# Neighbourhood attention: the values of four pairs of heads at once, by seven products of halves, with the modulation rows loaded singly and moved

## The chip, the cores and the metric

The kernel runs on one core of a Trainium2 chip, in one launch, all in float32. The core has a matrix engine (TensorE, PE in the profile; PEld is its loading of weights), a vector engine (VectorE, DVE), a scalar engine (ScalarE, ACT), GpSimd (unused here but for start-up) and SyncE (SP), whose queue issues every DMA of the kernel. Operands lie in the on-chip memory SBUF; TensorE writes to eight PSUM banks of 128 x 512. The metric is the device time of one launch in microseconds, the median of the timed runs.

## The reference

Two DiT-like layers and a third block on 256 latent tokens and 256 context tokens, width 1024. The change lies in the mixer of the second layer, which attends from each latent query to a grid window and to all context tokens:

```
def na_mixer(h, hc, w_qkv, rpb, w_o, need_ctx):
    H, d = 16, 64
    q = (h @ w_qkv[:, :1024])                       # latent tokens only
    k, v   = split((h  @ w_qkv[:, 1024:]), 2)       # 256 latent tokens
    kc, vc = split((hc @ w_qkv[:, 1024:]), 2)       # 256 context tokens
    s     = q k^T * d**-0.5 + bias(rpb), masked to the window
    s_ctx = q kc^T * d**-0.5
    p = softmax([s_ctx, s])
    y = (p[:ctx] @ vc + p[ctx:] @ v) @ w_o
```

Beside it, the kernel computes rows of the modulation (`ada_w`, a matrix times the conditioning vector c after SiLU) for later layers; 32 of these rows, each a dot product of 1024 with the 128 columns on the partitions, are done by VectorE in this stage.

## The kernel before

SBUF holds `A`, the layer input, transposed: 128 partitions x 8 steps of k (KT) x 512 tokens (T; columns 0 to 255, CTX, are context, the rest latent, LAT). Weights come through a ring of two slots of 6144 columns, filled by SP in the order of the table `STREAM`; a chunk may overwrite the chunk two before it when the semaphore in `CHUNK_USED` says so. SP's program (`sync_program`, `load_pairs`) is one queue in order: a wait in it holds up every issue behind it.

The stage `na_heads` goes over 8 pairs of heads (`NA_PAIRS`). Each pair has one chunk of 3072 columns: its query, key and value weights. TensorE's order (`na_heads_pe`, from L2158) is, for pair u: `scores(u)` (L2120, four products of 512 columns with 64 rows), `values(u)` (through the helper `mm`, L593: four tiles of 128 tokens, eight steps of k each, 128 columns wide), `keys(u+1)` (L2086, eight steps of 512 columns), `turn(u)` (L2127, 16 transposes of the normalized probabilities), `queries(u+1)` (L2082, eight steps of 256 columns) and `attend(u)` (L2138). In pair 0 half of the values stands ahead of the scores. In pair 7 there are no next keys; 12 products of the output projection (`out`, L2145) stand in their place, and two more behind `turn`. A float32 product counts as two instructions in the profile.

VectorE (`na_heads_dve`) does, for each pair: `maxima` (masking the bias, L2194; scaling the scores and adding the bias, L2204 and L2205; the maximum, L2209 and L2211), `normalize` (L2218, L2221), up to four or five modulation rows (`far`, L2229), two copies of turned tiles (`na_turned`, L2253), the copy of the next queries (L2186) and the copy of the attended output (L2245). ScalarE (`na_heads_act`) does the exponentials (L2268), copies values and keys out of PSUM (L2271, L2262) and copies two turned tiles. Everything is ordered by semaphores; `attend(u)` waits for both engines' copies of the turned tiles.

The modulation rows of this stage are loaded two at a time (`FAR_EACH`), 1024 KB, into three buffers (`load_far`, L420), each when the rows that were in the buffer are used. `FAR_PER_PAIR` says how many rows VectorE does in which pair. The biases of all 16 heads, 4 MB, lie in `N` and come in two parts (`load_biases`, L441), the first ahead of the second pair's chunk.

The stage before it (`ffn_split`) and others already compute products of two halves by seven in place of eight smaller products: sums and differences of blocks of the input and of the weights are formed by VectorE, seven products are made, and partial results are copied out of PSUM between products.

## Time and profile before

| | us |
|---|---|
| median of 3 timed runs | 1899.43 (1898.46 to 1900.1) |
| the profiled execution: its run | 1898.38 |
| the profiled execution: its span | 1896.5 |
| TensorE busy in the span | 1741.8 (92%), 14306 instructions |
| VectorE busy | 915.5 (48%) |
| ScalarE busy | 367.2 (19%) |
| mean granted TensorE clock | 0.969 |
| HBM read | 393.26 MB, mean 209 GB/s |

The page divides the span into 40 slices. TensorE is busy nine tenths or more from the second slice to the thirtieth, and six to eight tenths in the expert stage at the end, in which the DMA engines are busy throughout and the granted clock is 0.8. The neighbourhood attention lies in slices 16 to 20, from 715.6 to 908 us. Its products are known by their lines in the kernel, which the table of groups, the chain of waits and the timelines all name.

### The profile page before, as it was taken

The page shows a single profiled execution, that of the slowest core. Times are in us where ns is not written, and L with a number is a line of the kernel's source. Part 1 is how long each engine was busy: PE and PEld are TensorE (multiplying, and loading weights), DVE is VectorE, ACT ScalarE, POOL GpSimd, SP SyncE. Part 2 cuts the span into 40 slices and gives each one's busy share as a digit, 9 for nine tenths or more (in the row PEclk, how much of TensorE's full clock was granted, in tenths as well). Part 3 has the DMA queues.
Part 4 walks back from the last instruction along what each step waited for, and adds up shares of the span by engine and source line. Part 5 has one row for each costly group of instructions (what it writes and reads, how often), then busy time and mean ns, then how long its engine had stood idle before and what let it go on. Part 6 is the DMA issues. An engine that isn't in the chain of part 4 may idle for free.

```text
span 1896.5 us, 33550 instructions
## 1 busy us (share of the span) xinstructions
PE 1741.8 (92%) x14306; PEld 1370.3 (72%) x14306; DVE 915.5 (48%) x1948; ACT 367.2 (19%) x872; POOL 0.2 (0%) x4
## 2 busy tenths in 40 slices
PE   8999999999999999999999999999999876666666
PEld 4455687888888887777888888788888655445554
DVE  1488878666666426677544413478433211111112
ACT  0343413112110114222211102203422100000001
POOL 0000000000000000000000000000000000000000
PEclk9999999999999999999999999999999988888888
DMA  9523342222222217445334543313286999999997
GB/s 383 206 112 139 129 178 88 82 79 81 81 101 86 90 46 221 156 160 196 123 140 171 194 183 134 134 68 134 89 366 265 426 429 427 429 427 430 427 429 310
DMA packets 32947, 395.77 MB, mean 209 GB/s; under 512 B 3664, under 2 KB 6736, under 8 KB 9040
## 3 DMA queue, kind: packets, MB, share of 16 engines
q1 hardware_dynamic: 32848, 394.33, 52.0%
q8 instruction: 77, 1.26, 0.3%
q14 instruction: 22, 0.18, 0.0%
HBM read 393.26 MB, written 1.05 MB: 208 GB/s over the span
## 4 chain that ended last, share of the span: by engine, by line
PE 77%; DMA 18%; DVE 3%; issue 1%; ACT 1%; SPq 0%; DVEq 0%
PE bank L593 22%; PE bank L1873 13%; DMA ring<-w_moe 13%; PE bank L1582 8%; PE bank L646 5%; DMA arena<-w_moe 4%; PE bank L3347 3%; PE bank L2086 3%; PE bank L891 2%; PE bank L3113 1%; PE bank L2082 1%; PE bank L1192 1%; PE bank L800 1%; DMA ring<-w_ada 1%; PE bank L2440 1%; PE bank L1168 1%
## 5 line engine op out<-in xcount | busy, mean ns | idle before, releaser
L593 PE MATMUL bank<-layer_input,ring 128*128 128x256 f32 x1152 | 253.1, 380 | 0.0
L593 PEld LDWEIGHTS bank<-layer_input,ring 128*128 128x128 f32 x1152 | 217.3, 190 | 31.5 <-issue 2.7
L3347 PE MATMUL bank<-arena 128*32 128x128 f32 x2008 | 80.0, 325 | 50.1 <-DMA arena<-w_moe 49.6
L1582 PE MATMUL bank<-arena,ring 128*128 128x256 f32 x544 | 121.8, 380 | 1.1 <-DMA ring<-w_ffn_out 1.1
L1873 PE MATMUL bank<-arena 128*128 128x256 f32 x504 | 115.7, 379 | 0.0
L3499 DVE TENSOR_TENSOR arena<-arena,bank 128x128 f32<-128x128 f32 x32 | 9.2, 288 | 220.5 <-PE bank L3347 220.5
L1582 PEld LDWEIGHTS bank<-arena,ring 128*128 128x128 f32 x544 | 103.1, 190 | 15.8 <-DMA ring<-w_ffn_out 1.5
L3347 PEld LDWEIGHTS bank<-arena 128*32 128x32 f32 x2008 | 68.4, 131 | 61.8 <-DMA arena<-w_moe 58.9
L1873 PEld LDWEIGHTS bank<-arena 128*128 128x128 f32 x504 | 95.7, 190 | 13.2 <-DVE arena L2002 0.2
L646 PE MATMUL bank<-arena,ring 128*128 128x256 f32 x452 | 99.1, 380 | 0.8 <-DVE arena L2245 0.6
L646 PEld LDWEIGHTS bank<-arena,ring 128*128 128x128 f32 x452 | 85.5, 190 | 13.3 <-issue 1.0
L3347 PE MATMUL bank<-ring,arena 128*32 128x128 f32 x1920 | 68.0, 301 | 28.3 <-DMA ring<-w_moe 27.5
L593 PE MATMUL bank<-arena 128*128 128x128 f32 (+2 forms) x400 | 86.5, 370 | 2.2 <-DVE arena L3327 1.0
L3347 PEld LDWEIGHTS bank<-ring,arena 128*32 128x32 f32 x1920 | 58.6, 121 | 38.8 <-DMA ring<-w_moe 33.8
L593 PE MATMUL bank<-ring,layer_input 128*128 128x128 f32 (+2 forms) x576 | 80.9, 300 | 0.0
L593 PEld LDWEIGHTS bank<-ring,layer_input 128*128 128x128 f32 x576 | 69.8, 192 | 14.4 <-issue 13.4
L1873 PE MATMUL bank<-layer_input,ring 128*128 128x256 f32 x336 | 79.4, 379 | 0.0
L593 PEld LDWEIGHTS bank<-arena 128*128 128x128 f32 x400 | 56.3, 193 | 27.3 <-issue 26.5
L1873 PEld LDWEIGHTS bank<-layer_input,ring 128*128 128x128 f32 x336 | 63.8, 190 | 9.1 <-issue 0.5
L3464 DVE COPY arena<-bank 32x256 f32<-32x256 f32 x60 | 24.9, 415 | 88.5 <-PE bank L3358 88.1
L3464 ACT COPY arena<-bank 32x256 f32<-32x256 f32 x60 | 21.8, 363 | 215.2 <-PE bank L3358 214.8
L1935 DVE SCALAR_TENSOR_TENSOR arena<-arena,vectors 128x510 f32<-128x510 f32 x84 | 59.2, 747 | 5.1 <-DVE arena L1931 2.4
(507 smaller groups left out, 2662.9 us busy)
## 6 DMA issues: line engine op xcount, KB each, us to landing
arena<-w_moe SPq DMA_DIRECT2D x45, 2048.0 KB, 25.8
ring<-w_moe SPq DMA_DIRECT2D x45, 2048.0 KB, 26.6
ring<-w_ffn_in SPq DMA_DIRECT2D x22, 2048.0 KB, 7.8
ring<-w_ffn_out SPq DMA_DIRECT2D x8, 2816.0 KB, 9.9
ring<-w_proj SPq DMA_DIRECT2D x7, 3072.0 KB, 10.0
ring<-w_ada_late SPq DMA_DIRECT2D x8, 2560.0 KB, 9.1
ring<-w_na_pair SPq DMA_DIRECT2D x8, 1536.0 KB, 6.2
arena<-w_far SPq DMA_DIRECT2D x11, 1024.0 KB, 6.7
```

The costliest lines, as they stand in the source:

```text
L593: last = pe.matmul(out, a, b, start=(k == 0), stop=(k == len(lhs) - 1))
L646: last = eng.matmul(bank[oc % 2][:, 0:w], self.ring[g % 2][:, o:o + P], rhs(k), start=(k == 0), stop=(k == nk - 1))
L800: last = pe.matmul(out[32 * g:32 * g + 32, 0:n], cs[:, k, :], weights[:, k * width + g * n:k * width + (g + 1) * n], start=(k == 0), stop= ...
L891: ins = pe.matmul(bank[m][:, :], v["w_in"][:, (k * 6 + m) * P:(k * 6 + m + 1) * P], self.A[:, k, :], start=(k == 0), stop=(k == KT - 1))
L1168: pe.matmul(bank[2 + 2 * t + j][:, :], q[half[j], at], k[half[j], :], start=True, stop=False, skip_group_check=True)
L1192: last = pe.transpose(bank[n][:, i * P:(i + 1) * P], p[:, at:at + P], ident)
L1582: last = eng.matmul(out, w[:, k * P:(k + 1) * P], x[:, k, :], start=(start and k == 0), stop=(stop and k == half - 1), skip_group_check=True)
L1873: last = pe.matmul(out, w[:, k * P:(k + 1) * P], x[:, k, :], start=(start and k == 0), stop=(stop and k == 3), skip_group_check=True)
L1935: last = dve.scalar_tensor_tensor(out=seg(u[x], olo, ohi), in0=seg(src[x], ilo, ihi), scalar=self.V[:, bass.ds(cw + t * 2 * FT + col, 1)], ...
L2086: return pe.matmul(bank[1][:, :], slot(u)[:, D + k * P:D + (k + 1) * P], self.A[:, k, :], start=(k == 0), stop=(k == KT - 1))
L3347: ins = eng.matmul(bank[x][group[q], 0:P], xe[:, k, SLOTS * e:SLOTS * e + SLOTS], weight(e, first, last, (x * KT + k) * FE + q * P, P), st ...
L3464: last = copy(y[group[g], (g - e) % 4, :], bank[2][group[g], 0:256])
```

## The change

The values of four pairs are computed at once, as a product of all 512 tokens with 512 columns of weights. Tokens are split in context and latent, k in its lower and upper four steps, columns in two halves of 256 (two pairs each). With the input blocks A11, A12 (context, lower and upper k), A21, A22 (latent) and the weight blocks alike, VectorE forms four sums of the input (s1 to s4, once) and four of the weights (t1 to t4, for each group); TensorE makes seven products of four steps of k, 128 tokens and 256 columns, for each of two token tiles i and each of two groups g: `value(g, i, n)`. ScalarE copies partial results out of the bank between products (`snap`), and VectorE adds three combinations (`cross`, `far_right`). The 14 products of a group are spread over TensorE's order: those of the first group in pair 0, those of the second in pairs 1 to 4. The old `values` is gone, and with it ScalarE's copy of it.

The weights come in six chunks of 4096 columns (2048 KB) in place of eight of 3072: keys and queries of pairs 0 and 1, values of the first group, keys and queries of 2 and 3, values of the second group, then pairs 4 and 5, and 6 and 7. The modulation rows are loaded singly (512 KB) into four buffers, and done 12, 0, 4, 7, 5, 2, 2, 0 in pairs 0 to 7. The biases are held for 8 heads at a time: 2 MB behind the second chunk, and twice 1 MB inside the stage. The turned tiles go to banks 3 to 6, since bank 7 holds products.

The core of the diff:

```diff
-FAR_BUFFERS, FAR_EACH = 3, 2
-FAR_PER_PAIR = (0, 4, 4, 4, 5, 5, 5, 5)
+FAR_BUFFERS, FAR_EACH = 4, 1
+FAR_PER_PAIR = (12, 0, 4, 7, 5, 2, 2, 0)
...
-          ("na_pair", NA_PAIRS, 3072), ("na_o", 2, 4096),
+          ("na_pair", 6, 4096), ("na_o", 2, 4096),
...
+NA_VALUES = {"products_done": OPENED["products_done"] + len(HEAD_STEPS[0]),
+             "scalar_out": OPENED["scalar_out"] + len(HEAD_STEPS[2]),
+             "vector_in": OPENED["vector_in"] + 8 + 4 * 3, "vector_out": OPENED["vector_out"] + 4}
+VALUE_ORDER = [(0, 1), (0, 2), (0, 3), (0, 4), (0, 5), (0, 6), (1, 2), (0, 7), (1, 3), (1, 1), (1, 5), (1, 4), (1, 6), (1, 7)]
+VALUE_STEPS = len(VALUE_ORDER)
...
-    "na_pair": ("na_proj_done", each(1)), "na_o": ("y_ready", each(4, RESIDUAL_BASE["na_o"])),
+    "na_pair": ("na_qk_done", lambda c: 4 * c - 4), "na_o": ("y_ready", each(4, RESIDUAL_BASE["na_o"])),
...
-                if name == "na_pair" and first == 1:
-                    self.load_biases(sp, slice(0, 4), self.const_in)
...
+                    self.load_biases(sp, 0, slice(0, 8), self.const_in)
                     sp.wait_ge(self.sem("ffn0_up_used"), FT + 4)
-                    self.load_biases(sp, slice(4, 16), self.rest_in)
                     self.load_pairs(sp, load, g0)
...
+        values = NA_VALUES["products_done"]
+        chunk("na_qk_done", 4, 2)
+        rows(4, 12)
+        chunk("products_done", values + VALUE_STEPS, 3)
+        rows(12, 16)
+        sp.wait_ge(self.sem("na_biased"), 8)
+        self.load_biases(sp, 8, slice(0, 4), self.rest_in)
+        rows(16, 18)
+        chunk("na_qk_done", 8, 4)
+        rows(18, 20)
+        sp.wait_ge(self.sem("na_biased"), 16)
+        self.load_biases(sp, 8, slice(4, 8), self.rest_in)
+        rows(20, 28)
+        chunk("products_done", values + 2 * VALUE_STEPS, 5)
+        rows(28, FAR_LOADS)
...
+        def value(g, i, n):
+            w, at = self.na_value_weights(g), self.na_steps(g, i)
+            near, far = slice(i * P, i * P + P), slice(CTX + i * P, CTX + i * P + P)
+            low, high, far_high = self.A[:, 0:4, near], self.A[:, 4:8, near], self.A[:, 4:8, far]
+            s1, s2, s3, s4 = [x[:, :, near] for x in v["sums"]]
+            x, y, out, start = {1: (low, "lo0", left, True), 2: (high, "hi0", first_cross, True),
+                                3: (s1, "t1", second_cross, True), 4: (s2, "t2", left, False),
+                                5: (s4, "hi1", second_cross, False), 6: (s3, "t3", left, False),
+                                7: (far_high, "t4", left, False)}[n]
+            if (i, n) == (0, 1):
+                self.na_value_loaded(pe, g)
+            if n in (3, 4, 5, 6, 7):
+                pe.wait_ge(s["vector_in"], ready + ((0, 0, 0, 2, 4, 5, 7, 8), (0, 0, 0, 9, 10, 10, 11, 12))[g][n])
+            if n == 1 and (g, i) != (0, 0):
+                pe.wait_ge(s["scalar_out"], at["free"])
+            if n == 2 and (g, i) != (0, 0):
+                pe.wait_ge(s["vector_out"], at["pair_free"])
+            if n in (4, 5, 6, 7):
+                pe.wait_ge(s["scalar_out"], at[{4: "first", 5: "fifth", 6: "second", 7: "third"}[n]])
+            for k in range(4):
+                last = pe.matmul(out, x[:, k, :], w[y][:, k * CTX:(k + 1) * CTX], start=(start and k == 0), stop=(k == 3),
+                                 skip_group_check=True)
+            last.then_inc(s["products_done"], 1)
...
+        value(0, 0, 1)
+        value(0, 0, 2)
+        scores(0)
+        keys(1)
+        value(0, 0, 3)
+        value(0, 0, 4)
+        value(0, 0, 5)
+        queries(1)
+        value(0, 0, 6)
+        value(0, 1, 2)
+        turn(0)
+        value(0, 0, 7)
+        value(0, 1, 3)
+        value(0, 1, 1)
+        value(0, 1, 5)
+        value(0, 1, 4)
+        keys(2, 0, 3)
+        value(0, 1, 6)
+        keys(2, 3, 5)
+        value(0, 1, 7)
+        keys(2, 5, KT)
+        attend(0)
+        scores(1)
+        queries(2)
+        value(1, 0, 1)
+        value(1, 0, 2)
+        value(1, 0, 3)
+        keys(3, 0, 1)
+        turn(1)
+        value(1, 0, 4)
+        attend(1)
+        scores(2)
+        keys(3, 1, KT)
+        value(1, 0, 5)
+        value(1, 0, 6)
+        turn(2)
+        queries(3)
+        attend(2)
+        scores(3)
+        value(1, 1, 2)
+        keys(4)
+        value(1, 0, 7)
+        turn(3)
+        value(1, 1, 3)
+        queries(4)
+        value(1, 1, 1)
+        value(1, 1, 5)
+        attend(3)
+        scores(4)
+        value(1, 1, 4)
+        keys(5, 0, 5)
+        value(1, 1, 6)
+        keys(5, 5, KT)
+        value(1, 1, 7)
+        turn(4)
+        queries(5)
+        attend(4)
+        for u in (5, 6):
             scores(u)
-            values(u, (2, 3) if u == 0 else range(4))
-            if last:
-
-                pe.wait_ge(self.w_loaded[go % 2], 16 * (go // 2 + 1))
-                pe.wait_ge(s["o_used"], u)
-                out(0, range(KT - 1))
-                out(1, range(KT - 3))
-            else:
-                keys(u + 1)
+            keys(u + 1)
+            queries(u + 1, 0, 4)
             turn(u)
-            if last:
-                out(1, range(KT - 3, KT - 1))
-            else:
-                queries(u + 1)
+            queries(u + 1, 4, KT)
             attend(u)
+        scores(7)
+        pe.wait_ge(self.w_loaded[go % 2], 16 * (go // 2 + 1))
+        pe.wait_ge(s["o_used"], 7)
+        out(0, range(KT - 1))
+        out(1, range(KT - 3))
+        turn(7)
+        out(1, range(KT - 3, KT - 1))
+        attend(7)
...
+        def weight_sum(g, n, count):
+            w = self.na_value_weights(g)
+            if n == 1:
+                self.na_value_loaded(dve, g)
+            if n == 4:
+                dve.wait_ge(s["products_done"], self.na_value_done(g, 1, 2))
+            x, y = {1: ("lo1", "lo0"), 2: ("hi1", "t1"), 3: ("hi1", "lo1"), 4: ("hi0", "t2")}[n]
+            add(w[f"t{n}"], w[x], w[y], ALU.subtract, count)
...
+        def cross(g, i):
+            at, home = self.na_steps(g, i), self.na_value_homes(v, g, i)
+            dve.wait_ge(s["products_done"], self.na_value_done(g, i, 5))
+            dve.wait_ge(s["scalar_out"], at["second"])
+            if g == 1:
+                dve.wait_ge(s["o_done"], 2)
+            dve.tensor_tensor(home["c11"], bank[7][:, 0:CTX], v["first"], ALU.add).then_inc(s["vector_out"], 1)
+            dve.tensor_tensor(home["c12"], bank[7][:, CTX:2 * CTX], v["second"], ALU.add).then_inc(s["vector_out"], 1)
+        def far_right(g, i):
+            at, home = self.na_steps(g, i), self.na_value_homes(v, g, i)
+            dve.wait_ge(s["scalar_out"], at["third"])
+            dve.tensor_tensor(home["c22"], v["third"], v["fifth"], ALU.add).then_inc(s["vector_out"], 1)
...
+        dve.wait_ge(self.sem("mix_a_ready"), self.a_base + KT)
+        add(s1, A[1][0], A[1][1], ALU.add, 1)
+        weight_sum(0, 1, 2)
+        add(s2, s1, A[0][0], ALU.subtract, 3)
+        weight_sum(0, 2, 4)
+        maxima(0)
+        add(s4, A[0][1], s2, ALU.subtract, 5)
+        weight_sum(0, 3, 6)
+        add(s3, A[0][0], A[1][0], ALU.subtract, 7)
+        normalize(0)
+        cross(0, 0)
+        fars(0, 0, 1)
+        queries(1)
+        weight_sum(0, 4, 8)
+        fars(0, 1, 2)
+        turned(0)
+        far_right(0, 0)
+        fars(0, 2, 6)
+        cross(0, 1)
+        fars(0, 6, 8)
+        far_right(0, 1)
+        fars(0, 8, 12)
+        attended(0)
+        maxima(1)
+        weight_sum(1, 1, 9)
+        normalize(1)
+        weight_sum(1, 2, 10)
+        turned(1)
+        weight_sum(1, 3, 11)
+        queries(2)
+        attended(1)
+        maxima(2)
+        normalize(2)
+        cross(1, 0)
+        fars(2, 0, 2)
+        turned(2)
+        far_right(1, 0)
+        fars(2, 2, 4)
...
+        for u in (5, 6):
             maxima(u)
             normalize(u)
-            for i in range(min(FAR_PER_PAIR[u], 4)):
-                far(sum(FAR_PER_PAIR[:u]) + i)
-            self.na_turned(u, 0, s, v, dve, dve.tensor_copy, "pt_dve")
-            if FAR_PER_PAIR[u] > 4:
-                far(sum(FAR_PER_PAIR[:u]) + 4)
-            if u + 1 < NA_PAIRS:
-                queries(u + 1)
-            dve.wait_ge(s["o_done"], u + 1)
-            dve.tensor_copy(v["oT"][:, u * LAT:(u + 1) * LAT], bank[6][:, 0:LAT]).then_inc(s["o_used"], 1)
+            fars(u, 0, 2)
+            turned(u)
+            queries(u + 1)
+            attended(u)
+        maxima(7)
+        normalize(7)
+        turned(7)
+        attended(7)
...
+        snap(0, 0, "first")
+        keys(1)
+        snap(0, 0, "fifth")
+        soften(0)
+        snap(0, 0, "second")
+        act.wait_ge(self.cvec_in, 96)
+        act.activation(self.far_c(), self.far_c(), ACT.Silu).then_inc(self.sem("open_silu_ready"), 1)
+        snap(0, 0, "third")
...
-    W["na_pair"] = a["na_w_qkv"][0].reshape(KT, P, 3, NA_PAIRS, P).transpose(3, 1, 2, 0, 4)\
-        .reshape(NA_PAIRS, P, -1)
+    w = a["na_w_qkv"][0].reshape(KT, P, 3, NA_PAIRS, P)
+    qk = w[:, :, 0:2].reshape(KT, P, 2, 4, 2, P).transpose(3, 1, 4, 2, 0, 5).reshape(4, P, -1)
+    vw = w[:, :, 2].reshape(2, 4, P, 2, 2, CTX).transpose(3, 2, 0, 4, 1, 5).reshape(2, P, -1)
+    W["na_pair"] = np.stack([qk[0], vw[0], qk[1], vw[1], qk[2], qk[3]])
```

In ScalarE's order, the exponentials `soften(u)` and the copies `keys`, `turned` stand as before with the copies `snap` between them. `add` is one VectorE sum and a wait for it.

## Rows read from the trace of the kernel before

**Rows 1.** Windows: core, us, busy us (instructions) by engine, granted clock, DMA share, GB/s.
```profile
715.60:912.00 196.40, 195.43 (x1130) 140.84 (x1131) 137.71 (x270) 53.67 (x114) 0.00 (x0) 1.00 0.50 178
```

**Rows 2.** Chain of waits in the stage: start us, us, engine, line, instructions.
```profile
726.27 3.57 PE bank L593 x32
729.84 1.92 PE bank L2120 x8
731.75 3.77 PE bank L593 x32
735.52 6.87 PE bank L2086 x16
742.39 1.75 PE bank L2127 x16
744.14 3.46 PE bank L2082 x16
747.59 1.88 PE bank L2138 x16
...
751.39 7.34 PE bank L593 x64
```

**Rows 3.** Timeline of TensorE, first FFN: start us, us, engine, line, operation.
```profile
404.36 1.89 PE L1873 MATMUL bank<-arena 128*128 128x256 f32 x8
406.09 1.89 PE L1873 MATMUL bank<-layer_input,arena 128*128 128x256 f32 x8
```

**Rows 4.** VectorE's groups by form: line, operation, shapes, count, busy us, mean ns, idle.
```profile
L2229 DVE CUSTOM_DVE_ANT_0 arena<-arena,ring,vectors 128x1024 f32<-128x1024 f32 x22 | 27.3, 1280 | 0.0
...
L2765 DVE TENSOR_TENSOR residual<-arena 128x1024 f32<-128x1024 f32 x8 | 9.7, 1218 | 5.3 <-PE bank L2524 4.0 <-PE bank L2530 1.3
```

**Rows 5.** Timeline of TensorE, pair 7: scores and attend.
```profile
888.65 1.99 PE L2120 MATMUL bank<-arena 64*128 64x512 f32 x8
...
905.90 1.95 PE L2138 MATMUL bank<-arena 128*64 128x256 f32 x16
```

**Rows 6.** Timeline of VectorE, pair 7: the normalizing, then the copies.
```profile
897.49 0.88 DVE L2221 TENSOR_SCALAR arena<-arena,stats 128x512 f32<-128x512 f32 x2
...
898.89 0.88 DVE L2221 TENSOR_SCALAR arena<-arena,stats 128x512 f32<-128x512 f32 x2
...
904.52 1.28 DVE L2253 COPY arena<-bank 128x512 f32<-128x512 f32 x2
```

**Rows 7.** DMA issues: out<-in, queue, count, KB each, median us to landing.
```profile
ring<-w_ffn_in SPq DMA_DIRECT2D x22, 2048.0 KB, 7.8
...
arena<-w_far SPq DMA_DIRECT2D x11, 1024.0 KB, 6.7
```

**Rows 8.** DMA of w_ffn_in alone, its 22 issues.
```profile
DMA to landing us min/median/max: 7.5/7.8/8.6
```

**Rows 9.** DMA of w_na_o alone, its 2 issues.
```profile
DMA to landing us min/median/max: 8.8/9.8/10.7
```

**Rows 10.** Timeline of the DMA queue: issue us, us (of both), line.
```profile
881.41 0.33 SPq L420 DMA_DIRECT2D arena<-w_far  x1
881.78 16.55 SPq L328 DMA_DIRECT2D ring<-w_na_o  x2
```

**Rows 11.** Timeline of TensorE, expert stage and ahead of it; idle us before, releaser.
```profile
1452.24 3.81 PE L593 MATMUL bank<-arena 128*128 128x128 f32 x32 [1.05 <-DVE arena L3327]
...
1568.72 3.45 PE L3358 MATMUL bank<-arena 128*32 128x256 f32 x32 [2.14 <-DMA arena<-w_moe]
...
1578.43 2.94 PE L3347 MATMUL bank<-ring,arena 128*32 128x128 f32 x64 [2.94 <-DMA ring<-w_moe]
```

**Rows 12.** Windows of one us in the expert stage, columns as in rows 1.
```profile
1568.00:1569.00 1.00, 0.28 (x8) 0.24 (x12) 0.00 (x0) 0.00 (x0) 0.00 (x0) 0.99 1.04 442
1569.00:1570.00 1.00, 1.00 (x16) 0.68 (x12) 0.00 (x0) 0.00 (x0) 0.00 (x0) 0.50 1.08 459
...
1572.00:1573.00 1.00, 0.88 (x8) 0.54 (x4) 0.77 (x2) 0.73 (x2) 0.00 (x0) 0.80 0.92 393
```

More of the change, by code:

```diff
@@ new lines, in na_heads_dve, with add @@
+        ready_0 = NA_VALUES["vector_in"]
+        A = [[self.A[:, 4 * y:4 * y + 4, c:c + CTX] for y in range(2)] for c in (0, CTX)]
+        s1, s2, s3, s4 = v["sums"]
+        def add(out, x, y, op, count):
+            dve.tensor_tensor(out, x, y, op).then_inc(ready, 1)
+            dve.wait_ge(ready, ready_0 + count)
+        def weight_sum(g, n, count):
[6 more added lines that the diff above has]
+            add(w[f"t{n}"], w[x], w[y], ALU.subtract, count)
@@ new lines, in na_heads_dve @@
+        normalize(1)
[11 more added lines that the diff above has]
+        fars(2, 2, 4)
+        queries(3)
+        attended(2)
+        maxima(3)
+        weight_sum(1, 4, 12)
+        normalize(3)
+        fars(3, 0, 2)
+        turned(3)
+        fars(3, 2, 5)
+        queries(4)
+        fars(3, 5, 7)
@@ L2262, in keys, with soften @@
             act.copy(v[f"k{u % 2}"], bank[1][:, :]).then_inc(s["k_copied"], 1)
[L2263 to L2264 removed]
+        def soften(u):
             _, nb, rs, _ = v["stats"][u % 2]
```

197 lines of the change are left out of this document (136 added, 61 removed).

## The prediction

> **What bounds the kernel now.** The profiled execution spans 1896.5 us and its run took 1898.38 us; the median of the three timed runs is 1899.43 us, 1.05 us above it. I work out a difference and take it off the median. The change lies in one stage, the neighbourhood attention, so I read that stage and not the shares of the whole. First the table of windows [rows 1]: from 715.6 to 912 us TensorE is busy 195.43 of 196.40 us, at full clock (1.00, which is the 2.4 GHz level), while VectorE is busy 137.71 us. Then the chain of waits [rows 2]: from 726.27 us on it is TensorE work laid end to end, with no engine or DMA between. So the stage is as long as its TensorE instructions. A pair of heads takes 23.2 us: scores 1.92, values 7.34, keys 6.87, turn (the transposes) 1.75, queries 3.46, attend 1.88 [rows 2]. Whatever shortens TensorE's list is a full gain as long as nobody makes it wait. That second half is the question here, since the 7.34 us of values were also what TensorE did while the softmax of the pair ran on VectorE and ScalarE.
>
> **What is removed.** Values of pairs 0 to 7: 3.57 + 3.77 for pair 0 and 7 x 7.34 us for the others [rows 2], the same in each pair: 58.7 us for 256 products of 128 columns.
>
> **What is added on TensorE.** Per group of four pairs, 7 products x 2 token tiles x 4 steps of k = 56 products of 256 columns; two groups, 112. The kernel already has such products of four steps with a wait ahead of each: two of them start at 404.36 and 406.09 us, 1.73 us apart, or 0.432 us for one step [rows 3]. 28 x 1.73 = 48.4 us. TensorE's list gets 10.3 us shorter. Queries and keys keep their number and shape. From here I lay the new lists of the three engines beside each other, in the order of the diff, with these durations, and start TensorE's first value product at 726.2 us. The same walk over the old order ends attend of pair 7 at 907.9 us; in the trace it starts at 905.90 and lasts 1.95 us [rows 5].
>
> **What is added on VectorE.** Four sums of halves of the input and eight of the weights, 128x1024 each: 12 x 1.22 us, as the nearest form takes [rows 4], with a wait behind each some 1.27. Twelve combinations of 128x256, about 0.4 us each. Together 20 us on an engine that has 59 us free in the stage, so the total is no bound; the places are what counts. In pair 0 VectorE copies the queries (726.8), makes four sums (731.9), the maxima (738.5), three sums (742.3), so that t1, t2, s4, s3 are ready at 729.4, 731.9, 739.8 and 742.3 us. TensorE wants them at 738.5, 740.2, 741.9 and 747.1 us. It has scores and the keys of pair 1 ahead of them, and waits for none. The last weight sum (t4) ends at 751.9 us and is wanted at 752.3: cover 0.4 us, and if it goes, the wait costs what it is late. Priced at nothing, kept with +-0.5.
>
> **The modulation rows.** Still 32, of 1.2 us each when they follow one another (22 of them were busy 27.3 us) [rows 4], 12 of them now in pair 0, where TensorE has 47 us of work (14 value products, two keys, scores, queries, turn, attend). VectorE is done with them at 770.9 us and attend of pair 0 ends at 773.2. Each is loaded alone, at 512 KB, where a 1024 KB row load took 6.7 us in the median [rows 7]; the fourth later row is needed more than 3.9 us after its issue in my walk, and VectorE has 2.3 us to spare at the end. Nothing for TensorE. In pairs 5 and 6 two rows stand between the softmax and VectorE's copies of the turned tiles. There the cover is gone: normalizing ends 11.1 us after the scores start (888.65 to 899.77) [rows 5, 6], two rows make 13.5, the two copies (1.28 us together from 904.52) [rows 6] make 14.9, and attend may start at 15.0. TensorE is there at 1.92 + 6.87 + 3.46 + 1.75 = 14.0. **A wait of 0.9 us, twice.** With values it was 21.3.
>
> **Pair 7** has nothing in place of its values but the 12 early products of the output projection, 5.2 us. The first normalized tile comes 9.3 us after the scores start (888.65 to 897.97), the last 11.1 [rows 5, 6]; TensorE is at turn after 1.92 + 5.2 = 7.1. It waits 2.1 us, then 0.6 inside turn. Less the 0.2 us that the old order waits before its last attend: **+2.5 us.**
>
> **The loads.** Weights now come as 2048 KB chunks, at fewer places. SP issues in order, so I follow its queue. Chunk 0 and the first value chunk are asked for before the stage, the latter now ahead of the biases; the copy of c, biases and rows behind it are 4.5 MB where there were 7.5 MB. Chunk 2 is issued at 747.2 (queries of pair 1 done) and needed at 761: hidden. The second value chunk, issued 768.8, needed 778.6 by TensorE: hidden, by 9.7 against 7.8. **Chunk 4 is not.** It waits for the queries of pair 3, and between their end and the keys of pair 4 TensorE has only attend 1.88, scores 1.92 (0.2 late for the copy of the queries) and one product of 1.73, 5.7 us. A 2048 KB load took 7.8 us in the median of 22 [rows 7], 7.5 to 8.6 [rows 8]; 8.8 and 10.7 in the two of the output weights [rows 9], the first of which is issued 0.4 us behind a row load [rows 10]. With 7.8 and 0.1 us for SP and TensorE each the wait is **2.6 us**, and 0.2 at the scores; with 8.8 it is 3.6, with 10.7 5.5. I take 7.8 since the two rows ahead of chunk 4 are issued 3.6 and 2.4 us before it and are 512 KB only. Chunk 5 is issued at about 850.0, behind a row load and the last product of the second group, and wanted at 858.9: 8.9 us, hidden at 7.8, 1.8 us of wait at 10.7. Biases of pairs 4 to 7 are issued 50 us before their use. The Trainium skill ("DMA: Bandwidth & Descriptors", Anatomy of one DMA) fits one DMA as 2.0 us and the bytes at 436 GB/s; that makes 6.8 us here, an estimate by that page, and by it the wait would be 1.6 and the gain 1.0 us larger. The rows, 22 of them at 7.5 or more, decide for the longer time.
>
> **The clock.** The old stage has no gap. The new one has one of 2.6 us before the keys of pair 4 and one of 2.1 (with 0.6 close behind) in pair 7. What a gap does is seen in the expert stage: TensorE had stood for 2.14 us at 1568.72 and for 2.94 at 1578.43 [rows 11]; around the first the granted clock was 0.99 in the microsecond from 1568 and 0.50 in the one from 1569 (the 1.2 GHz level), with 0.80 in that from 1572 [rows 12], so low for some 3.4 us, in which half the work is lost: 1.7 us. The 1.05 us before 1452.24 [rows 11] are the nearest gap on the other side, and TensorE had worked densely up to it. 2.6 and 2.1 are nearer to the longer gaps, but the work ahead of those is thinner than here. I count one such stretch, +1.7, with 0 and 3.4 as bounds.
>
> **The sum.** -10.3 + 2.6 + 0.2 + 1.8 + 2.5 = -3.2 us without the clock, -1.5 with one low stretch. 1899.43 - 1.5 = 1897.9 us. The own range of this case is 1895.5 to 1900.5.
>
> **Rivals.** A measurement of this kernel tells about 0.2% (3.8 us) from no change.
> (1) *The clock holds.* Then 1899.43 - 3.2 = 1896.2. For it: dense products around the gap. Against: both gaps of [rows 11] over 2 us. It is within 0.2% too.
> (2) *The chunks come late, and it is slower.* SP's queue holds row loads ahead of chunks 4 and 5 and rows behind. If they cost as [rows 9] shows at its long end, 10.7 us, the waits are 5.5 (keys of pair 4), 2.2 (keys of pair 6), 1.4 (first product of the second group), 0.4 at scores, 0.9 and 2.5: 12.9, a loss of 2.6 us, and with two or three low stretches 6 to 8: about 1905.5. It decides from a landing of 9.8 us on (9.3 with one low stretch). Against it: the rows ahead are half as large as the one in front of that row.
> (3) *The waits are mostly not there.* If chunk 4 is hidden and the rows of pairs 5 and 6 cost nothing, only pair 7's 2.5 is left: 1899.4 - 7.8 = 1891.6. For it: none of the new waits is in the trace, and my walk has some 90 places where a landing or a copy can come sooner than I count. Against: 5.7 us of cover is less than the shortest of the 22 landings, 7.5.
> (4) *The products don't run at 0.432.* The old values take 7.34 / 32 = 0.229 us for 128 columns, 0.459 for 256. At that pace 112 products take 51.4 us, the gain on the list is 7.3 in place of 10.3, and the time 1900.9. Against: [rows 3].
>
> **Chances.** Forecast with one low stretch 0.42, (1) 0.22, (2) 0.12, (3) 0.14, (4) and other added waits of some us 0.10. Faster by over 0.2% is (3) and the lucky end of (1): 0.18. Slower by over 0.2% is (2) and a little of (4): 0.12. Within: 0.70. The range takes in forecast, (1), (4) and the bounds of landing and clock: 1894.9 to 1901.9.
>
> **What would show it.** In the new trace: value products 1.73 us apart per four steps; keys of pair 4 waiting for a DMA of na_pair, 2.6 us; attend of pairs 5 and 6 waiting 0.9 us for VectorE's copies; turn of pair 7 waiting 2.1 us for VectorE; a granted clock of 0.50 for some us behind the keys' wait or not; no wait for a sum in pair 0; everything after the stage shifted by one amount. The prediction is wrong if the 2048 KB loads land in other than 7.5 to 8.8 us, if VectorE falls behind in pair 0, or if a wait stands at a product that I counted as covered.

## The result, and the profile after

The changed kernel takes 1902.07 us (median of 20 runs, 1900.58 to 1905.76), the kernel before 1898.66 us (20 runs beside them): ratio 1.0016, 95% interval 1.001 to 1.0022. It is slower by some 3.4 us where -1.5 us were forecast, and its time is 0.2 us above the upper end of the range of the forecast. The profiled execution spans 1899.5 us (before 1896.5).

The page of the changed kernel: TensorE's busy time (PE), and the granted clock by slice.

```profile
PE 1734.4 (91%) x14018; PEld 1357.6 (71%) x14018; DVE 932.5 (49%) x1972; ACT 370.3 (19%) x884; POOL 0.2 (0%) x4
...
PEclk9999999999999999999999999999999988888888
```

TensorE is busy 7.4 us less in the whole span and the span is 3.0 us longer. The windows of the stage, which answer to [rows 1]:

```profile
714.70:912.00 197.30, 188.09 (x835) 125.39 (x836) 154.28 (x292) 56.76 (x126) 0.00 (x0) 0.99 0.52 172
```

In place of 1 us TensorE now stands 9.2 us, and the clock is 0.99 instead of 1.00. The timeline of TensorE (start us, us, line, shapes, in brackets the wait ahead and who ended it) shows the new products and every wait of 0.2 us or more up to the output projection:

```profile
746.29 1.89 PE L2188 MATMUL bank<-ring,arena 128*128 128x256 f32 x8
748.01 1.89 PE L2188 MATMUL bank<-ring,layer_input 128*128 128x256 f32 x8
...
785.26 1.09 PE L2207 MATMUL bank<-constants,arena 128*128 128x128 f32 x8 [0.25 <-DVE arena L2362]
786.79 1.99 PE L2188 MATMUL bank<-ring,arena 128*128 128x256 f32 x8 [0.43 <-DVE ring L2391]
...
817.06 8.83 PE L2145 MATMUL bank<-layer_input,ring 128*128 128x512 f32 x16 [3.90 <-DMA ring<-w_na_pair]
...
876.04 1.95 PE L2221 MATMUL bank<-arena 128*64 128x256 f32 x16 [0.73 <-DVE arena L2500]
...
892.89 1.95 PE L2221 MATMUL bank<-arena 128*64 128x256 f32 x16 [0.72 <-DVE arena L2500]
...
904.13 1.09 PE L2207 MATMUL bank<-constants,arena 128*128 128x128 f32 x8 [1.99 <-DVE arena L2362]
905.54 1.09 PE L2207 MATMUL bank<-constants,arena 128*128 128x128 f32 x8 [0.32 <-DVE arena L2362]
```

From top to bottom: two value products 1.72 us apart; two waits in pair 1 that nobody had forecast; the keys of pair 4 behind the DMA of chunk 4, and 8.83 us long instead of 7.13; attend of pairs 5 and 6; the two halves of the turn of pair 7. I measure the stage from here on between the first value product and the first product of the output projection: **182.36 us before (726.10 to 908.46), 184.78 after (725.22 to 910.00)**. Summed by kind, from each group's start to the next one's less the wait (an instruction that waits inside a group counts with the group):

| us in the stage | before | after | 
|---|---|---|
| values | 58.09 | 49.10 |
| keys | 48.07 | 50.37 |
| turns | 13.99 | 14.68 |
| scores, queries, attend, output products | 61.60 | 61.67 |
| waits | 0.61 | 8.96 |
| sum | 182.36 | 184.78 |

So +2.4 us come from the stage. The start of the stage lies 0.9 us earlier, which is within the scatter (725.2 to 727.0 in the profiles of the changed kernel and its variants), and the time behind it is 988.04 us before and 989.50 after; that difference is looked at behind the experiments.

Windows of one us from 817 us on, behind the wait of 3.90 us (the column behind the last "(x0)" is the granted clock):

```profile
817.00:818.00 1.00, 0.94 (x2) 0.49 (x3) 0.47 (x2) 1.00 (x5) 0.00 (x0) 0.94 1.18 365
818.00:819.00 1.00, 1.00 (x2) 0.34 (x1) 0.96 (x3) 1.00 (x3) 0.00 (x0) 0.50 0.95 152
...
821.00:822.00 1.00, 1.00 (x3) 0.38 (x3) 1.00 (x3) 0.00 (x0) 0.00 (x0) 0.85 1.05 238
```

The clock is 0.50, the 1.2 GHz level, from 818 to 821 us and 0.85 in the next one; the keys take 1.70 us more. In pair 7, behind 1.99 us of standing, it stays 1.00.

SP's queue around chunk 4 (issue us, us, line), and what it loaded (KB each, us to landing):

```profile
803.60 1.54 SPq L424 DMA_DIRECT2D arena<-w_far  x2
807.47 0.33 SPq L334 DMA_DIRECT2D ring<-w_na_pair  x1
807.84 1.24 SPq L424 DMA_DIRECT2D ring<-w_far  x2
...
ring<-w_na_pair SPq DMA_DIRECT2D x1, 2048.0 KB, 9.5
```

And pair 1 on ScalarE:

```profile
779.87 0.37 ACT L2527 COPY extra<-bank 128x256 f32<-128x256 f32 x1 [8.64 <-PE bank L2188]
780.26 1.28 ACT L2514 ACT_TABLE_LOAD   x1
781.55 0.72 ACT L2514 ACTIVATE arena<-arena,stats 128x512 f32<-128x512 f32 x1
```

The maxima of pair 1 are ready at 779.45 us (VectorE, L2352). ScalarE stands before its copy of the first product of the second group, comes to the exponentials behind it, and only then loads their table, 1.28 us: the first exponential starts at 781.55, 2.1 us late. In the kernel before nothing stood ahead of the exponentials, and the table was loaded at 747.15 us while ScalarE waited for the maxima.

### The profile page after: what moved, and what is told of

It reads as the page before. It is cut to its first block, busy times and chain, and to the rows that moved or that the text cites. A ratio compares the mean times of both kernels' runs of the same rounds, so it can differ in the third digit from the quotient of the medians.

```text
span 1899.5 us, 33068 instructions
## 1 busy us (share of the span) xinstructions
PE 1734.4 (91%) x14018; PEld 1357.6 (71%) x14018; DVE 932.5 (49%) x1972; ACT 370.3 (19%) x884; POOL 0.2 (0%) x4
## 4 chain that ended last, share of the span: by engine, by line
PE 74%; DMA 20%; DVE 4%; ACT 1%; issue 1%; SPq 0%; DVEq 0%; ACTq 0%
PE bank L615 19%; DMA ring<-w_moe 18%; PE bank L1895 13%; PE bank L1604 9%; PE bank L668 5%; PE bank L3647 3%; PE bank L2188 2%; PE bank L2145 2%; PE bank L913 2%; PE bank L3413 1%; PE bank L2141 1%; PE bank L1214 1%; DMA ring<-w_ada 1%; PE bank L822 1%; PE bank L2740 1%; PE bank L1190 1%
## 5 line engine op out<-in xcount | busy, mean ns | idle before, releaser
L2145 PE MATMUL bank<-layer_input,ring 128*128 128x512 f32 x128 | 60.4, 613 | 4.3 <-DMA ring<-w_na_pair 3.9
L1492 DVE TENSOR_SCALAR arena<-bank,vectors 128x256 f32<-128x256 f32 x44 | 21.9, 539 | 75.2 <-PE bank L615 68.8
```

The source lines that it names most:

```text
L1492: ins = eng.tensor_scalar(dst, src, self.V[:, bass.ds(cw + 2 * FT + col, 1)], self.V[:, bass.ds(cb + col, 1)], ALU.mult, ALU.add)
L2145: return pe.matmul(bank[1][:, :], weights(u, 1)[:, k * P:(k + 1) * P], self.A[:, k, :], start=(k == 0), stop=(k == KT - 1))
```

## Experiments

Each run stood beside runs of the kernel before on its own chip. All edits but that of run 5 are made to the changed kernel; runs 9, 11 and 12 start from the orders of run 8. Waits, landings and stages come from one profiled execution of each kernel.

**1. The exponentials of pair 1 first.**

```diff
-        snap(1, 0, "first")
         soften(1)
+        snap(1, 0, "first")
```

> One edit of the changed kernel: in ScalarE's order of pair 1 the copy of the first partial result of the second group stands behind the four exponentials, not ahead of them. My theory: in the changed kernel the table for the exponentials is loaded only behind that copy (780.26 us, 1.28 us), so the exponentials start 2.1 us after the maxima are ready and TensorE waits in turn of pair 1 and before the product behind it. Then the table is loaded while ScalarE waits, the first exponential starts within 0.1 us of the maxima, the two waits of TensorE in pair 1 go, and the stage (first value product to the first product of the output projection, 184.8 us) takes 183.4 us; the whole some 1.4 us less, 1900.7. Rival: the wait in pair 1 comes from VectorE's weight sums, not from the exponentials; then the stage stays at 184.8.

Measured: 1901.31 us, ratio 1.0009 (1.0000 to 1.0019). Both waits of pair 1 are gone, and from the scores of pair 1 to those of pair 2 it takes 16.96 us in place of 18.18: 1.22 us won. But the stage is 185.85 us, 1.1 longer than before the edit: chunk 4 landed in 10.7 us, the keys of pair 4 waited 5.05 us and took 9.96. The issue of chunk 4 moved with TensorE:

```profile
806.82 0.33 SPq L334 DMA_DIRECT2D ring<-w_na_pair  x1
```

That is 81.0 us behind the first value product where it was 82.3 us, so the 1.2 us arrive there whole. The longer landing took them back. The edit leaves the queue around chunk 4 as it was, and with two rows just ahead of it chunk 4 landed in anything from 9.5 to 12.3 us (six profiles). So the term is real, and this profile hides it. The ratio is 0.0007 lower than that of the changed kernel (1.3 us, where 1.4 were expected), but the two intervals overlap.

**2. TensorE kept busy before the keys of pair 4.** 17 products of the identity into an idle bank.

```diff
         value(1, 1, 2)
+        self.fill(pe, 17, bank[0])
         keys(4)
```

> One edit of the changed kernel: 17 products of the identity into a free bank stand before the keys of pair 4, where TensorE waited 3.9 us for its weights. They compute nothing that is used. Theory (the clock is a cost of its own): the keys still start when their chunk lands, 5.8 us after the product before, but the granted clock stays at 1.00, the keys take 7.1 us and not 8.8, and the stage takes 183.1 us in place of 184.8. Rival (the low clock is only the record of the wait, and what follows has slack): the stage stays at 184.8, or grows if the products outlast the wait.

Measured: 1900.93 us, ratio 1.0008 (0.9998 to 1.0017). The fill runs 3.96 us, the keys take 7.13 us again, with 0.18 us of wait. Then the clock fell in pair 7, behind 2.00 us of standing:

```profile
902.80 1.09 PE L2207 MATMUL bank<-constants,arena 128*128 128x128 f32 x8 [2.00 <-DVE arena L2363]
904.21 1.97 PE L2207 MATMUL bank<-constants,arena 128*128 128x128 f32 x8 [0.31 <-DVE arena L2363]
905.97 1.74 PE L2228 MATMUL bank<-arena,ring 128*128 128x256 f32 x4
```

Half a turn takes 1.97 where it took 1.09, four products 1.74 where they took 1.03; the granted clock from 904 to 905 us is 0.50. The stage is 184.72 us: one low stretch went, another came.

**3. Chunk 4 asked for earlier.** Queries of pair 3 ahead of two value products and the turn of pair 2; chunk 4 ahead of the row loads 16 to 18.

```diff
         keys(3, 1, KT)
+        queries(3)
         value(1, 0, 5)
         value(1, 0, 6)
         turn(2)
-        queries(3)
...
-        rows(16, 18)
         chunk("na_qk_done", 8, 4)
-        rows(18, 20)
+        rows(16, 20)
```

> One part of the changed kernel undone: the queries of pair 3 stand ahead of two value products and the turn of pair 2, and the DMA queue issues the chunk of pairs 4 and 5 ahead of two row loads. The work is the same. Theory: the chunk is issued some 5.3 us earlier and lands before TensorE asks for it, so the wait of 3.9 us and the low clock behind it (1.7 us) go: stage 184.8 - 5.6 = 179.2 us, the whole about 1896.5, under the kernel before. Rival: what is late next (the row loads, the weight sum t4 or the softmax of pair 3) takes the place of the wait; then the stage stays above 182.

Measured: 1899.03 us, ratio 0.9996 (0.9987 to 1.0006), stage 182.69. Chunk 4 is issued at 802.53 us and lands in 8.2; no wait at the keys, full clock. Two waits take its place, since VectorE's order was left as it was:

```profile
808.88 1.95 PE L2220 MATMUL bank<-arena 128*64 128x256 f32 x16 [1.19 <-DVE arena L2499]
811.85 1.99 PE L2199 MATMUL bank<-arena 64*128 64x512 f32 x8 [1.02 <-DVE arena L2326]
```

attend of pair 2 waits for copies of turned tiles, scores of pair 3 for the copy of the queries, which stands behind rows. In pair 7 the clock fell, behind 2.00 us of standing. The stage was to be 179.2 us; the rival, which said that something else would be late and the stage stay above 182, describes it better.

**4. The rows of pairs 5 and 6 moved to pairs 3 and 4.**

```diff
-FAR_PER_PAIR = (12, 0, 4, 7, 5, 2, 2, 0)
+FAR_PER_PAIR = (12, 0, 4, 9, 7, 0, 0, 0)
```

VectorE's order has the same four rows moved.

> One part of the changed kernel undone: the four modulation rows that VectorE does in pairs 5 and 6 are done in pairs 3 and 4 (12, 0, 4, 9, 7, 0, 0, 0). Theory: the two waits of 0.73 us before attend of pairs 5 and 6 go, stage 183.3 us; some tenths may come back where pair 4's copies are later. Rival: pair 3 and 4 have no room, since each row needs its load; then TensorE waits there by 1 us or more and the stage is not shorter.

Measured: 1913.3 us, ratio 1.0066 (1.0049 to 1.0083), stage 196.20: far off. attend of pairs 5 and 6 wait no longer, but

```profile
871.19 2.08 PE L2200 MATMUL bank<-arena 64*128 64x512 f32 x4 [7.87 <-DVE arena L2327]
...
865.59 1.28 DVE L2370 CUSTOM_DVE_ANT_0 arena<-arena,extra,vectors 128x1024 f32<-128x1024 f32 x1 [6.98 <-DMA arena<-w_far]
...
840.86 0.33 SPq L424 DMA_DIRECT2D ring<-w_far  x1
856.27 0.33 SPq L334 DMA_DIRECT2D ring<-w_na_pair  x1
856.64 0.91 SPq L424 DMA_DIRECT2D arena<-w_far  x2
```

Read from below: SP issues row 27 at 840.86 us and then stands for chunk 5 until 856.27; the next row loads are behind it in the queue; VectorE, which now wants them in pair 4, waits 6.98 us; the copy of the queries stands behind the rows, and the scores of pair 5 wait 7.87 us. I moved work on VectorE and left its loads where they were.

**5. Single row loads in the kernel before.**

```diff
-FAR_BUFFERS, FAR_EACH = 3, 2
+FAR_BUFFERS, FAR_EACH = 4, 1
```

The addresses of the buffers follow.

> The kernel before with one edit: modulation rows loaded singly (512 KB, four buffers) in place of two at a time, everything else as it was. Theory A: single row loads cost nothing by themselves; the stage from the first value product to the output projection stays 182.4 +- 0.3 us (before 182.36), and the ratio is 1.000 +- 0.0007. Theory B: their smaller packets (4 KB per partition) slow the stream also where there is room; then some rows come late at VectorE and the stage grows by 1 us or more. It also gives a second reading of the time behind the stage: 988.04 us in the profile of before, 989.1 to 990.2 in the five profiles of the changed kernel and its variants. If it belongs to the profile and not to the kernel, it will read 989 or more here; if to the changed kernel, 988.

Measured: 1913.92 us, ratio 1.0078 (1.0062 to 1.0093), stage 196.19. Neither theory foresaw it. One wait, and the low clock on the products behind it (7.47 us for 5.34), make it:

```profile
909.20 7.47 PE L2146 MATMUL bank<-arena,ring 128*128 128x256 f32 x24 [11.74 <-DMA ring<-w_na_o]
...
884.38 16.43 SPq L421 DMA_DIRECT2D ring<-w_far  x2
900.86 0.91 SPq L328 DMA_DIRECT2D ring<-w_na_o  x2
```

With four buffers of one row the last row load waits for the first row of pair 7 (a buffer comes free), and the output weights behind it in SP's queue are issued at 900.86 us where they were issued from 881.78 on [rows 10]. Up to there no wait is added, so smaller loads alone cost TensorE nothing there; the place at which the queue has to wait for a buffer does. In the changed kernel the hand-written queue issues these weights at 859.27 us.

**6. Two rows taken from behind chunk 4; 7. two rows taken from ahead of it.**

```diff
         rows(16, 18)
         chunk("na_qk_done", 8, 4)
-        rows(18, 20)
         sp.wait_ge(self.sem("na_biased"), 16)
+        rows(18, 20)
```

> The changed kernel with two row loads (18, 19) moved out from behind chunk 4 to behind the next wait of SP's queue, so that nothing shares the DMA engines with chunk 4 but the two rows ahead of it. Theory A (the rows behind it make it late): landing 8.2 us in place of 9.5, the wait at the keys of pair 4 falls from 3.90 to 2.6 us and the low clock stays; stage 183.5 us against 184.78. Theory B (the two rows ahead make it late, or the landing is just spread): landing 9.2 or more, wait 3.6 or more, stage 184.5 or more.

```diff
-        rows(16, 18)
         chunk("na_qk_done", 8, 4)
-        rows(18, 20)
+        rows(16, 20)
```

> The changed kernel with the two row loads ahead of chunk 4 (16, 17) moved behind it, TensorE's order untouched. So far the 2048 KB loads of this stage landed in 9.5 and 9.6 us where two rows had been issued in the 4 us ahead of them, with two rows behind or without, in 9.2 and 10.4 in another such place, and in 7.7 to 8.2 with rows only behind. Theory A (512 KB ahead of a chunk delay it as they share the engines with its first part): landing 8.0, wait at the keys of pair 4 2.4 us, stage 183.3 us, or 181.6 if the clock then holds. Theory B (the place in the stage, not the rows): landing 9.5, stage 184.8.

Measured (a single run of each, so no ratio): stage 184.82 and 183.20 us, time 1901.51 and 1900.54 us. Landing, first with nothing behind the chunk, then with nothing ahead of it:

```profile
ring<-w_na_pair SPq DMA_DIRECT2D x1, 2048.0 KB, 9.6
...
ring<-w_na_pair SPq DMA_DIRECT2D x1, 2048.0 KB, 8.0
816.13 8.83 PE L2144 MATMUL bank<-layer_input,ring 128*128 128x512 f32 x16 [2.33 <-DMA ring<-w_na_pair]
```

The rows ahead make it late, those behind don't: both edits leave TensorE's order alone, and only the second brings the landing down. The same over chunks 2 to 5 of the changed kernel and all its variants, 48 loads of 2048 KB, by what SP had issued in the 4 us ahead:

| row loads in the 4 us ahead | loads | us to landing |
|---|---|---|
| none (up to four close behind) | 31 | 7.5 to 8.4 |
| one, 1.9 us ahead | 7 | 8.2 to 8.7 |
| two | 10 | 8.8 to 12.3 |

With a landing of 8.0 us the wait is 2.33 us; the forecast had 2.6 for 7.8. The clock fell all the same (0.50 from 818 to 820 us): 2.33 us of standing was enough.

**8. The orders mended together; 9. with a fill in pair 7.** Exponentials of pair 1 first (run 1); on TensorE in pair 2 queries(3), turn(2), value(1, 0, 6), attend(2); chunk 4 ahead of rows 16 to 20; and on the other engines:

```diff
-FAR_PER_PAIR = (12, 0, 4, 7, 5, 2, 2, 0)
+FAR_PER_PAIR = (12, 0, 3, 7, 6, 2, 2, 0)
...
-        fars(2, 0, 2)
+        fars(2, 0, 1)
+        queries(3)
+        fars(2, 1, 2)
         turned(2)
         far_right(1, 0)
-        fars(2, 2, 4)
-        queries(3)
+        fars(2, 2, 3)
...
-        fars(4, 3, 5)
+        fars(4, 3, 4)
         queries(5)
+        fars(4, 4, 6)
...
-            fars(u, 0, 2)
             turned(u)
             queries(u + 1)
+            fars(u, 0, 2)
...
+        turned(2)
         snap(1, 0, "third")
-        turned(2)
```

> The changed kernel with orders only altered: exponentials of pair 1 ahead of the first copy of a partial product; queries of pair 3 ahead of the turn of pair 2, chunk 4 issued behind them and ahead of the rows; a product between the turn and attend of pair 2; VectorE's rows of pairs 5 and 6 behind its copies of the turned tiles and of the queries; one row from pair 2 to pair 4. Theory A (my account: the change loses by places, not by its products): no wait at the keys of pair 4 with a landing of 8.2 to 10, none at attend of pairs 2, 5 and 6, pair 1 without its 0.68 us of waits; left is the wait in pair 7, now 3 us (TensorE comes there earlier with VectorE where it was), with one low stretch of the clock; stage 177.5 us with it, 176 without, time 1895 (0.9975 of before). Theory B (VectorE or the loads become the bound as TensorE gets faster): new waits for copies of queries or for rows of 2 us or more in pairs 3 and 4, stage 180 or more, no gain on before.

Measured: 1895.95 us, ratio 0.9979 (0.9970 to 0.9988), stage 178.15. No wait for a DMA, none at attend; 2.28 and 0.32 us in pair 7 are left, at full clock. The stage is 6.6 us shorter than in the changed kernel, with the same products. It was to be 176 us at full clock; of the 2.1 us more, 1.8 are in three scores, which take longer than the 1.99 us of the others, those of pairs 5, 6 and 7; the first:

```profile
855.78 2.58 PE L2199 MATMUL bank<-arena 64*128 64x512 f32 x8
```

> The same, and nine 128x128 products of the identity into an idle bank ahead of the turn of pair 7, where TensorE stands 2 to 3 us. Theory A (the low clock in pair 7 comes from the stand, and costs some 1.6 us): granted clock 1.00 there, stage 1.6 us shorter than in the kernel without them if that one shows low clock in pair 7, equal (+- 0.3) if that one does not. Theory B (the clock has another cause, heat or load of the whole stage): it falls with the fill as well.

Measured: 1895.02 us, ratio 0.9977 (0.9966 to 0.9987), stage 179.69. Clock 1.00 in pair 7, as without the fill; chunk 5 landed in 10.4 us in this profile and the keys of pair 6 waited 0.88, and the scores of pair 4 were long as well; these two make the 1.5 us by which the stage is longer than in run 8. The two theories aren't told apart by it, as run 8 kept its clock.

**10. Both stands of the changed kernel filled.**

```diff
+        self.fill(pe, 17, bank[0])
         keys(4)
...
+        self.fill(pe, 9)
         turn(7)
```

> The changed kernel with idle products in both long stands of TensorE: 17 before the keys of pair 4 and 9 before the turn of pair 7, so that no low clock stretch is left in the stage while all waits stay. Theory A (low clock follows the stands, and the price is 1.6 to 2.0 us of the stage): stage 183.0 +- 0.4 against 184.72 with the first fill alone (clock fell in pair 7) and 184.78 with none (clock fell at the keys of pair 4). Theory B (a fall moves on to another place): stage 184.5 or more with a low stretch elsewhere.

Measured: 1900.83 us, ratio 1.0004 (0.9994 to 1.0013). The profiled execution misses both theories: chunk 4 landed in 12.3 us, TensorE waited 2.85 us behind the fill, the keys took 8.76 us at low clock, stage 187.45. In pair 7 the clock held, with 0.31 us of wait left. Its ratio can't be told from run 2's, so what both fills together give is not settled by it, nor is theory B of this run, that a fall only moves. The profiles leave that open too. Where the clock fell at the keys of pair 4 it held in pair 7 behind 1.99 to 2.00 us (the changed kernel, runs 1, 6 and 7), and where it held there, it fell in pair 7 (runs 2, 3 and 11); run 4, with falls at both, and run 8, with none, break the pattern.

**11. One edit of run 8 undone.** ScalarE's first copy ahead of the exponentials of pair 1 again.

> The kernel with the altered orders (178.15 us of stage, 0.9979 of before) with one of its edits undone: ScalarE's first copy of a partial product of the second group stands ahead of the exponentials of pair 1 again, as in the changed kernel. Theory A (the order costs 1.4 us of waits in pair 1 and nothing downstream takes the gain back here): stage 179.5 us, waits of 0.25 and 0.43 at the turn of pair 1 and the product behind it, ratio 0.9986. Theory B (the gain is absorbed downstream also here): stage 178.2, ratio 0.9979.

Measured: 1896.95 us, ratio 0.9983 (0.9973 to 0.9993), stage 180.42. From the scores of pair 1 to those of pair 2 18.17 us against 16.95: 1.22 us, as in run 1, and here nothing takes it back. The other 1.06 us are the clock in pair 7, which fell in this profile:

```profile
899.46 3.57 PE L2206 MATMUL bank<-constants,arena 128*128 128x128 f32 x16 [2.27 <-DVE arena L2361]
```

A stand of 2.27 us ahead of it, against 2.28 in run 8 where the clock stayed 1.00.

**12. A row put where VectorE stood.** In pair 5 of run 8 VectorE waits 1.47 us between the copies of the turned tiles and of the queries, and the copy of the attended output, for which the last product of the scores waits, is behind two rows. With the fill of run 9:

```diff
             turned(u)
+            fars(u, 0, 1)
             queries(u + 1)
-            fars(u, 0, 2)
+            fars(u, 1, 2)
```

> The kernel with the altered orders and the fill in pair 7, with one more place mended: in the two profiles of it, the scores of pairs 5, 6 and 7 take 2.58 us in place of 1.99, since their last product waits for VectorE's copy of the attended output, which stands behind two modulation rows; before it VectorE stands 1.47 us between its copies of the turned tiles and of the queries. In pairs 5 and 6 one of the two rows now goes into that stand. Theory A (the stretch comes from the second row): scores of pairs 6 and 7 1.99 us again, stage 1.2 us shorter, 176.9 us with full clock and without a wait for chunk 5 (1 us more with one like the 0.88 of the last look), ratio 0.9972. Theory B (the copy of the queries now comes late, or something else is next): stage 178 or more, ratio as before, 0.9978.

Measured: 1892.46 us, ratio 0.9959 (0.9945 to 0.9973), stage 176.70 where 176.9 was expected.

```profile
854.24 2.58 PE L2199 MATMUL bank<-arena 64*128 64x512 f32 x8
870.89 1.99 PE L2199 MATMUL bank<-arena 64*128 64x512 f32 x8
886.95 1.99 PE L2199 MATMUL bank<-arena 64*128 64x512 f32 x8
```

The scores of pair 5, ahead of which stand the rows of pair 4 that were not touched, stay at 2.58; pairs 6 and 7 are at 1.99. This version is the fastest of all. Against the kernel before its median is 8 us lower (5 runs, so 5 to 10 us by the interval); its stage is 5.7 us shorter and its profiled span 5.3, and what lies beyond that in the median is not explained.

**What isn't settled.** The time behind the stage is 987.7 to 988.0 us in three profiles (before, run 5, run 10) and 989.0 to 990.2 in the eleven others. The difference lies in the last 67 us: counted back from the end, the fifth last 128x128 transpose of the expert stage starts 64.6, 65.2 and 65.1 us ahead in the three, 67.0 to 67.5 in the eleven. There the products wait for the experts' weights (some 430 GB/s up to 1870 us), and the last such wait stands ahead of a group of 64 products on a ring load. In the eleven TensorE stands 2.3 to 2.6 us there and this group takes 2.9 to 3.6 us (3.61 at 1869.15 us in the changed kernel), and so does the group of 64 before it; in the three it stands 0.7 to 0.9 us, both groups take 1.95, and the low clock lay one group earlier. Run 10 has the changed kernel's instructions and the shorter form, so none of the change's does it; why one form or the other comes was not found. It is up to 1.5 us of the 3.4. With the stage's 2.4, less the 0.9 us of the earlier start, that makes the 3.0 us by which the profiled span grew.

## Why the prediction was wrong

The forecast for the stage was -1.5 us, the profile shows +2.4. The 3.9 us between them are 2.7 in TensorE's list and 1.25 in the waits (8.35 more than before, forecast 7.1); the clock's term, 1.7, is 1.70. So three steps failed: the sizes in the list, the wait of pair 1 put at nothing, and the landing of chunk 4. Two of the prediction's own signs of being wrong came true: a landing outside 7.5 to 8.8 us, and a wait at a product counted as covered.

- **The list** was to get 10.3 us shorter and got 7.6 (values 58.09 to 49.10, keys 48.07 to 50.37 less 1.70 of clock, turns 13.99 to 14.68, the rest +0.07). Four sizes were off, by 0.6 or 0.7 us each. The old values are 58.09 us from start to start where I took 58.7 from the durations of [rows 2]. The new ones run at 1.72 us, nearly as [rows 3] said, but the 28 of them take 49.1 and not 48.4. So rival (4) is out as a cause, though the 7.6 us that the list gave are near its 7.3. The keys take 0.6 us more (0.54 in run 8). That isn't for being cut in pieces: uncut ones are longer too, and those of pair 5, cut in two, take 4.29 + 2.57 = 6.86 us as before. It is 0.10 us in each of six pairs, and goes by the neighbour; in pair 4 that is a stand, in the others scores or attend. Keys of pair 2 before, behind values, and of pair 6 after, behind scores, each with its next instruction:

```profile
781.78 7.03 PE L2086 MATMUL bank<-layer_input,ring 128*128 128x512 f32 x16
788.64 1.91 PE L2127 MATMUL bank<-constants,arena 128*128 128x128 f32 x16
...
862.97 7.13 PE L2145 MATMUL bank<-layer_input,ring 128*128 128x512 f32 x16
869.94 1.89 PE L2141 MATMUL bank<-layer_input,ring 128*128 128x256 f32 x8
```

From start to start 6.86 and 6.97 us. What stands directly behind scores, or directly ahead of scores or attend, is 0.09 to 0.11 us longer where no wait is beside it, the values and queries too; in the order before, the values stood behind the scores and bore it. I took the whole of the old values off, border included. Three such borders are also 0.3 of the 0.7 us in the new values; most of the rest is at two products beside a wait, in pairs 1 and 4. The 0.7 us in the turns are two that stand in halves with a wait between, in pairs 1 and 7.
- **Pair 1** was priced at nothing: the step that failed most plainly. It costs 1.22 us (runs 1 and 11): 0.68 as waits at TensorE, the rest as the halved turn and the product behind it, which are in the list above. I followed VectorE's queue and SP's through the pair and took ScalarE's exponentials as ready with the maxima. The diff puts a copy that waits for a product ahead of them, and the table load of 1.28 us, which the kernel before did while waiting, cannot start until that copy is done.
- **Chunk 4**: the place, the cover (5.7 us) and the rule (landing less cover) held; the landing was 9.5 us and not 7.8, so 3.90 us of wait and not 2.6. I had a row for it, the 8.8 us of [rows 9], whose shorter load is issued 0.4 us behind a row load [rows 10], and set it aside since the rows ahead are half as large. Run 7 shows that they count: 8.0 us without them. Rival (2) was said to decide from 9.3 us on with one low stretch; 9.5 is past it, and the kernel is slower. Of its other waits, at the keys of pair 6, the first product of the second group and the scores, none came.
- **The Trainium skill** ("DMA: Bandwidth & Descriptors", Anatomy of one DMA) gave 6.8 us for such a load, an estimate by its fit. The page states that fit for DMAs issued by GpSimd, and these are issued by SyncE, which I didn't say; the traces have 7.5 to 8.4 us with nothing just ahead and up to 12.3 behind rows. Going by the rows rather than by the page was right, and didn't go far enough.
- **attend of pairs 5 and 6**: 0.73 and 0.72 us, forecast 0.9 each. **Pair 7**: 1.99 and 0.32, forecast 2.1 and 0.6. **Scores of pair 3**: no wait, forecast 0.2. **Pair 0**: no wait for a weight sum, with a cover of some tenths of a us as forecast: the sum ends at 751.17 us and is wanted at 751.49. The second value chunk and chunk 5: hidden, as forecast.
- **The clock**: one low stretch, where it was expected, at the price expected. That it stays 1.00 behind the 2 us of pair 7 was not certain: 1.99 to 2.0 us of standing left it at 1.00 in the changed kernel and in runs 1, 6 and 7, and it fell in runs 2, 3 and 4; 2.27 us in run 11 made it fall, 2.28 in run 8 not.
- Behind the stage I expected a shift by one amount. It is one amount (+1.55 us) up to about 1465 us and not in the expert stage; see what isn't settled.

## What to carry to other kernels

Fewer products are a gain only if each piece of the new order finds its input: the same products gave 1.0016 in the order of the change and 0.9959 in a mended one (with nine idle products added in a stand), and most of the 8.1 us of stage between them hung on places in queues (a copy ahead of the exponentials, rows ahead of a chunk, rows ahead of a copy). When an order of one engine is rewritten, follow all four queues through it, ScalarE's table loads included, and when work moves, move its loads with it, or TensorE waits for them, 7.87 us in run 4. A changed number of buffers moves the queue's waits as well: 11.74 us in run 5. And one profile of an edit of 1 us can be upset by one long landing, as in run 1: compare the piece that was edited, the issue behind it and the ratio, and not only the length of the stage.

## What the runs showed of the hardware

- A 2048 KB load is late behind small ones issued just ahead (8.8 to 12.3 us behind two), not beside ones issued after it (7.5 to 8.4). The two 512 KB loads ahead of chunk 4 took 3.9 us in the changed kernel and the two right behind it 12.7 (means of the two).
- After equal stands of 2.0 us (and of 2.3) in pair 7 the granted clock fell to 0.50 in some profiles and stayed 1.00 in others. Behind 2.33 us or more at the keys of pair 4 it fell in each of the six profiles that had such a stand; a fall in the stage cost 1.1 to 2.9 us.
- Products that stand directly behind scores (64 rows) or ahead of scores or attend (64 columns) took some 0.10 us more from start to start than the same ones elsewhere, in the kernel before and in its variants.
- The expert stage ran in two forms of its last 67 us, from the same instructions; the time behind the stage differs by 1.0 to 2.5 us with it.
